# Decode attention scores as 32-row products on keys turned by VectorE, with half of the paged latents gathered by index

## What is computed

```
kv latent cache (N_POOL pages, 128 tokens, 256), rope cache (N_POOL, 128, 32), page_table (8, 32), all float32
ckv, kr  = pages of the 8 sequences            # 8 x 4096 tokens x (256 + 32)
q_lat    = q_nope (8 seq, 8 tok, 6 heads, 64) . w_uk            -> (.., 256)
s_past   = (q_lat . ckv + q_rope . kr) * scale                  # over 4096 tokens
s_new    = the same against the 8 new tokens, causal mask
pr       = softmax([s_past, s_new])
o_lat    = pr . [ckv, ckv_new];   out = o_lat . w_uv
```

## Time and profile before

| | us |
|---|---|
| median of 3 runs (2025.14 to 2026.98) | 2026.8 |
| the profiled execution | 2029.75 |
| its span | 2028.1 |
| decode stage, first transpose (465.3) to the next stage's first DMA (733.3) | 268 |
| PE busy over the span | 1869.0 (92%) |
| mean granted TensorE clock, of full speed | 0.946 |

### The profile page before, as it was taken

One profiled execution on the slowest core, in us unless ns is written; L12 is line 12 of the kernel. 1 busy time (PEld: TensorE's weight loads), 2 busy tenths in 40 slices (PEclk: granted clock), 3 DMA queues, 4 the chain that ended last, 5 costly groups with the idle time before them and its releaser, 6 DMA issues. The chain is left out here.

```text
span 2028.1 us, 39649 instructions
## 1 busy us (share of the span) xinstructions
PE 1869.0 (92%) x16034; PEld 1641.6 (81%) x16034; DVE 978.9 (48%) x1800; ACT 513.8 (25%) x1064; POOL 255.0 (13%) x440
## 2 busy tenths in 40 slices
PE   5999998998999965999898979999999999999997
PEld 5999984665666632888746979999999999999996
DVE  6232426673455547544245335545545535445455
ACT  5111123542323333223124321111111111111113
POOL 1000004324444302000002210000000000000000
PEclk8999998998999966999867989999999999999999
DMA  7111113104555400000031111021021121110202
GB/s 231 53 42 53 40 43 83 31 10 130 154 155 153 124 25 0 4 4 4 18 132 53 32 32 42 22 73 37 27 63 42 31 64 32 42 53 24 64 21 111
DMA packets 148258, 119.19 MB, mean 59 GB/s; under 512 B 22900, under 2 KB 136298, under 8 KB 147805
## 3 DMA queue, kind: packets, MB, share of 16 engines
q1 hardware_dynamic: 138189, 97.35, 16.4%
q0 software_dynamic: 9744, 18.78, 3.4%
q10 hardware_dynamic: 144, 0.52, 0.1%
HBM read 102.81 MB, written 11.44 MB: 56 GB/s over the span
## 5 line engine op out<-in xcount | busy, mean ns | idle before, releaser
L202 PE MATMUL bank<-normed2T_hi,w_hi 128*128 128x384 f32 (+1 forms) x1056 | 346.0, 328 | 4.3 <-DVE w_lo L492 4.3
L203 PE MATMUL bank<-normed2T_hi,w_lo 128*128 128x384 f32 (+1 forms) x1056 | 345.7, 327 | 0.0
L204 PE MATMUL bank<-normed2T_lo,w_hi 128*128 128x384 f32 (+1 forms) x1056 | 345.7, 327 | 0.0
L202 PEld LDWEIGHTS bank<-normed2T_hi,w_hi 128*128 128x128 f32 x1056 | 199.1, 189 | 5.5 <-DVE w_lo L492 5.5
L203 PEld LDWEIGHTS bank<-normed2T_hi,w_lo 128*128 128x128 f32 x1056 | 199.0, 188 | 0.0
L204 PEld LDWEIGHTS bank<-normed2T_lo,w_hi 128*128 128x128 f32 x1056 | 199.0, 188 | 0.0
L202 PE MATMUL bank<-inner_hi,w_hi 128*128 128x384 f32 (+1 forms) x528 | 174.4, 330 | 10.2 <-DVE w_lo L492 7.1
L492 DVE TENSOR_TENSOR w_lo<-work,w_hi 128x1024 fp32r<-128x1024 f32 (+2 forms) x120 | 118.6, 989 | 131.1 <-ACT w_hi L487 129.9
L204 PE MATMUL bank<-inner_lo,w_hi 128*128 128x384 f32 (+1 forms) x528 | 174.1, 330 | 0.0
L203 PE MATMUL bank<-inner_hi,w_lo 128*128 128x384 f32 (+1 forms) x528 | 173.6, 329 | 0.0
L202 PE MATMUL bank<-normedT_hi,w_hi 128*128 128x384 f32 (+3 forms) x480 | 157.6, 328 | 5.5 <-DVE w_lo L492 5.5
(11 more groups left out here) (411 smaller groups left out, 3348.3 us busy)
## 6 DMA issues: line engine op xcount, KB each, us to landing
work<-in_w_up_dram SPq DMA_DIRECT2D x44, 512.0 KB, 3.8
residualT<-in_cache_kv_latent_dram SPq DMA_DIRECT2D x80, 128.0 KB, 2.5
residualT<-in_cache_kv_latent_dram POOLq DMA_DIRECT2D x80, 128.0 KB, 2.6
work<-in_w_in_dram SPq DMA_DIRECT2D x19, 512.0 KB, 3.8
work<-in_w_down_dram SPq DMA_DIRECT2D x32, 256.0 KB, 2.8
weight_ring<-in_cache_kv_latent_dram POOLq DMA_DIRECT2D x48, 128.0 KB, 2.7
weight_ring<-in_cache_kv_latent_dram SPq DMA_DIRECT2D x48, 128.0 KB, 2.5
residualT<-residual_spill SPq DMA_DIRECT2D x1, 4352.0 KB, 15.0
```

Of the source, the lines that this page charges most:

```text
L202: pe.matmul(out, w[0], x[0], start=first, stop=False)
L203: pe.matmul(out, w[1], x[0], start=False, stop=False)
L204: return pe.matmul(out, w[0], x[1], start=False, stop=last)
```

## The change

- **Keys.** PE no longer transposes the keys. DVE `turn_keys(j)` transposes each slot of load j in place of it, in blocks of 32x32, SBUF to SBUF: two instructions of [128, 1024] and two of [128, 128] per load, two loads ahead of the step that uses them.
- **Scores.** With 32x32 blocks turned, the 32 partitions of a page hold 32 of the 256 latents of its tokens at a time. `dscores` becomes 9 blocks (8 of latents, 1 of rope) x 4 pages q x 2 halves f = 72 products with 32 rows of contraction, 64 columns of queries and 128 columns of keys; page q writes bank q, and successive steps use different 128-column parts of the banks. The small step has 9 x 2 x 2 = 36 such products of 32 columns.
- **Queries.** They are stored as `q_blk`: each block of 32 latents repeated in all four groups of 32 partitions, scaled by SCALE already. `w_uk` is spread so that PE forms the repeated blocks: 48 products of 64 rows by 128 columns in place of 12.
- **Softmax.** DVE forms the negated maximum in one instruction, so the instruction L1450 goes. `copy_weights` and `copy_part` move from DVE to ACT; ACT's key copies go.
- **Loads.** SP issues only the four latent pages of half 0. POOL gathers, with indirect DMAs of 128 rows each, the latents of half 1 (4 KB a row) and the rope rows of both halves (512 B a row): three instructions per load in place of seven. Row numbers are computed on POOL in four small instructions at the start of the attention stage. The gather of rope rows waits for `k_t` of load j - 5, that of latents for `do_mm` as before. In the attention stage POOL's share of the early loads goes to the rounds q = 8 to 11: one gather in even rounds, two in odd ones.
- The table of pages goes to all partitions; some small copies of new keys are replaced by one transpose.

The core of the diff:

```diff
+        def load_pages(eng, j):
+            x, g = loads[j]
+            for q in range(4):
+                at_ = x * NPAGE + 4 * g + q
+                page = eng.value_load(pages[0:1, at_:at_ + 1], min_val=0, max_val=NPOOL - 1)
+                eng.dma_start(kslot[2 * (j % NL)][32 * q:32 * q + 32],
+                              kv_pages[bass.ds(page, 1)].rearrange("a p c -> (a p) c")).then_inc(s_k[0][j % NL], 16)
+        def gather_latents(pool, j, f):
+            x, g = loads[j]
+            b = x + NX * f
+            pool.indirect_dma_start(kslot[2 * (j % NL) + f], None, kv_rows,
+                                    bass.IndirectOffsetOnAxis(row_at[:, b, g:g + 1], 0)).then_inc(s_k[f][j % NL], 16)
...
             @block.gpsimd
             def _(pool):
-                all_loads(pool, 1)
+                for j in range(EARLY, len(loads)):
+                    if j >= NL:
+                        pool.wait_ge(k_t, 2 * (j - NL) + 2)
+                    for f in range(2):
+                        gather_ropes(pool, j, f)
+                    if j >= NL:
+                        pool.wait_ge(do_mm, step_of(j - NL) + 1)
+                    for f in (1,):
+                        gather_latents(pool, j, f)
...
+                    for b in range(KB):
+                        for q in range(4 if g < NG else 2):
+                            rows = slice(32 * q, 32 * q + 32)
+                            for f in range(2):
+                                out = PS[q][HD * f:HD * f + HD, P * (s % 2):P * (s % 2) + P]
...
+                                last = pe.matmul(out, q_blk[rows, b, x, f, :], keys, start=(b == 0),
+                                                 stop=(b == KB - 1), skip_group_check=True)
...
                 for s in range(NSTEP):
                     x, g = steps[s]
-                    following = s + 1 < NSTEP and steps[s + 1][1] < NG and steps[s + 1]
                     dscores(s)
                     if g == JOINED and x >= 1:
                         turn_joined(x - 1)
-                        pe.wait_ge(j_cp, x)
-                    if following:
-                        turn_keys(following[0] * NG + following[1], 0)
                     if s >= 1:
-                        dvalues(s - 1, 0)
-                    if following:
-                        turn_keys(following[0] * NG + following[1], 1)
+                        dvalues(s - 1)
                     turn_weights(s)
-                    if s >= 1:
-                        dvalues(s - 1, 1)
...
+                def turn_keys(j):
                     if j >= 2:
                         dve.wait_ge(ds_mm, step_of(j - 2) + 1)
+                    for f in range(2):
+                        slot = 2 * (j % NL) + f
+                        dve.wait_ge(s_k[f][j % NL], (64, 16)[f] * (j // NL + 1))
+                        dve.transpose(key_t[:, j % 2, f, 0:4 * RANK], kslot[slot])
+                        dve.wait_ge(s_kr2[f][j % NL], 16 * (j // NL + 1))
+                        dve.transpose(key_t[:, j % 2, f, 4 * RANK:KT], krr[:, slot, :]).then_inc(k_t, 1)
...
+                dve.wait_ge(s_nm, 16)
+                turn_keys(0)
+                turn_keys(1)
                 for s in range(NSTEP):
                     x, g = steps[s]
-                    following = s + 1 < NSTEP and steps[s + 1][1] < NG and steps[s + 1]
                     softmax_max(s)
-                    for half in range(2):
-                        if following:
-                            copy_keys(following[0] * NG + following[1], half)
-                    copy_weights(s)
-                    if s >= 1:
-                        copy_part(s - 1)
+                    if g < NG and x * NG + g + 2 < len(loads):
+                        turn_keys(x * NG + g + 2)
```

More of the change, by code:

```diff
@@ L984, in _ @@
                 pool.wait_ge(s_kr[1], 1)
+                pool.wait_ge(s_pg, 16)
+                for r in range(4):
+                    rows = slice(32 * r, 32 * r + 32)
+                    nc.gpsimd.tensor_scalar(row_at[rows], pages[rows].rearrange("p (b g r) -> p b g r", b=NB, r=4)[:, :, :, r],
+                                            32.0, C("page_row")[rows], ALU.mult, ALU.add).then_inc(s_ra, 1)
+                pool.wait_ge(s_ra, 4)
                 for q in range(NQ):
@@ new lines, in _ @@
+                for m in range(3):
+                    pe.wait_ge(wu_cp[m], 1)
+                    for b in range(KB - 1):
+                        for f in range(2):
+                            r = slice(HD * f, HD * f + HD)
+                            last = pe.matmul(PS[2 * m + f][:, b * NS:(b + 1) * NS],
+                                             w_uk_b[r, m, b].rearrange("p q c -> p (q c)"), qn[r, m, SEQ:T],
+                                             start=True, stop=True)
+                    last.then_inc(ql_mm, 1)
@@ L1252, in _ @@
-                act.wait_ge(s_q0, 2)
-                latent_queries(nc.scalar.copy, 1)
+                act.wait_ge(wu_t, 4)
+                spread_w(nc.scalar.copy, 1).then_inc(wu_cp[1], 1)
+                rope_queries(nc.scalar.mul, (0, 1))
+                for m in range(3):
+                    act.wait_ge(ql_mm, m + 1)
+                    latent_queries(nc.scalar.mul, 2 * m + 1)
         if upto == "queries":
@@ L1287, in build, with scores_of @@
         y_mm = sem("decode_values_ready")
-        with nc.Block() as block:
-            def all_loads(eng, f):
-                for j in range(EARLY, len(loads)):
-                    if j >= NL:
-                        eng.wait_ge(do_mm, step_of(j - NL) + 1)
-                    load_rows(eng, j, f)
+        def scores_of(s):
+            x, g = steps[s]
+            n, w = (4, P) if g < NG else (2, 32)
+            by_bank = banks8[:, 0:n * 512].rearrange("p (q w) -> p q w", q=n)
+            return by_bank[:, :, P * (s % 2):P * (s % 2) + w]
+        with nc.Block() as block:
             @block.sync
```

322 lines of the change are left out of this document (131 added, 191 removed).

## The result

The changed kernel takes 1998.2 us (median; 1996.7 to 2001.4) where the kernel before took 2026.9 in the same comparison: a ratio of 0.9862 with a 95% interval of 0.9845 to 0.9879. That is 28.7 us less, where 74 had been forecast. The profiled execution has a span of 1999.6 us.

A forecast was written before the change was run, and what follows sets the result against it. PE was taken to bound decode, busy 64.31 of 66 us. Steps -75, start of decode -3 and +1, queries +2.5, attention +0.5 gave -74 us: median 2026.8 to 1953 us, range 1936 to 2016.

The forecast's parts named there:

- Scores: Decode stage on PE: 144 records of 128 columns at 14.2 ns, 2.1 us per step, between 1.9 and 3.9.
- four tiles at once: Rival on decode scores: no more than four tiles work together, scores 3.9 us, PE's step 6.3, 1995 us; chance 0.13.
- the rows don't overlap: Slower rival on scores: only two column halves work at once, 7.7 us, step 10.1, 2115 us; 0.05 shared with falling clock.
- PE's step of 4.5 us: Full decode step by PE alone: scores 2.1, change of shape 0.1, chain 1.77, and 0.53 us.
- POOL sets the pace: Rival in decode: gathers of 1.6 to 2.3 us; at 1.96 the step is 6.2 us, 1991 us; chance 0.13.
- the gathers cost more than a step: Slower rival in decode: at 2.6 us per gather on POOL the step is 8.1 us, 2055 us; chance 0.09.
- The step of 5.0 us: Full decode step: 4.8 us mean from PE and DVE's joins plus 0.2 for mutual waits; 7.34 before, saving 75 us.
- the rival in which the clock falls: Slower rival: PE's idle times drop its clock to 1.2 GHz, step near 9 us, 2080 us; 0.05 shared with non-overlapping rows.
- Queries stage: PE does 96 records, not 24, two overlapping, 5.1 us; with spread and end copies +2.5 us (0 to +5).
- Start of decode: DVE turns load 0 in 3.0 us before first scores, previously at 6.2: -3 us; slow clock at start +1.
- Attention stage: POOL's row numbers and early gathers: round 9 needs 3.8 us against 3.58, +0.5 us (up to +4).
- Wrong it is if PE waits on DVE: Sign against the forecast: PE waiting on DVE in plain decode steps, or scores above 2.5 us.

## Why the prediction was right and wrong

The direction, and most of the prices, were right. 1998.2 us lies in the range, in its upper part, and 45 us above the point. The change gained 28.7 us of the 74 forecast.

- **Scores.** 2.1 us were forecast, for eight tiles working at once and a record every 14.2 ns. Without loads, and without the gathers alone, 144 records start within 2.05 us: the price was right for the array. In the changed kernel, beside the gathers, it was 2.34 in the median of the steps without a stop, 0.3 more, and the prediction had nothing for that. The rivals "four tiles at once" and "the rows don't overlap" are out. So is, for these tiles, the 25 ns of the Trainium skill that the prediction had weighed against the trace.
- **PE's step of 4.5 us.** The shortest steps without loads took 4.50 us, and two loads at once 9.65: right as what PE can do.
- **DVE.** 1.22 and 0.29 us were forecast for a turning. All 40 + 24 large ones have 1218 and 1219 ns, and the small ones 269:

```profile
L1430 DVE STREAM_TRANSPOSE work<-residualT 128x1024 f32<-128x1024 f32 x40 | 48.7, 1218 | 2.8 <-DMA residualT<-in_cache_kv_latent_dram 2.0 <-PEq L160 0.8
L1432 DVE STREAM_TRANSPOSE work<-residualT 128x128 f32<-128x128 f32 x64 | 17.2, 269 | 0.0
L878 POOL DMA_INDIRECT residualT<-in_cache_k_rope_dram,mixedT x64 | 61.6, 963 | 27.2 <-issue 15.6 <-POOLq L160 8.3 <-DVE work L1432 3.4
```

- **POOL.** A gather was put at 1.3 us (0.5 to 2.4); it takes 0.96, with 0.30 before the next: 3.8 us per load. The rivals "POOL sets the pace" and "the gathers cost more than a step" are out; what the gathers do to PE is a way that no rival had. All gathers of the decode stage took 0.94 to 1.20 us, though DVE turned keys beside them.
- **The step of 5.0 us: the step that failed.** The sum went through PE's work, DVE, SP, POOL and the DMA engines, and added 0.2 us for their entanglement. It had no term for the arrival of PE's instructions, of which the change takes 328 per step where there were 122. The forecast was 32 x 5.0 + 3 x 3.5 = 170.5 us from the first scores to the last small step's, and 212.6 came: 42 of the 45 us. Stops for instructions are 22.9 of the 42. Scores that start 0.3 us slower beside the gathers make some 9 (an estimate, 32 x 0.3, from the steps at full clock with and without them). The rest, some 10, is left for the lower clock and the waits for ACT; no run separates these. So the step failed by what its sum put at nothing: above all the arrival of instructions, then the slower start of the scores and the lower clock.
- **The clock.** 1.00 was forecast for the stage. A part of the rival in which the clock falls came true: 0.90 and 0.97 in the two windows, and 0.50 for 32 us of the 212.6, 12 of them at the start of the stage and the others each behind a long stop of PE.
- **Queries stage: mis-sized.** 96 x 53 ns = 5.1 us were forecast because alternating halves of the rows would overlap. 96 records took 10.50 us at a granted clock of 0.50, 109 ns each; in another kernel the same 96 took 5.58 at 1.00, 58 ns each. So one follows the other at either clock. That is weights of 128 columns and no overlap of the halves, as for the 24 records of the earlier trace rows, which should have been taken as they were. The Trainium skill, TensorE: Matmul & The Clock Gate, section "LDWEIGHTS (loading the stationary operand)", says that a weight load's time goes by its columns and not by its rows, columns/1.2 in ns: 107 ns for 128. At half clock the trace agrees; at full clock it shows 58. With that rule the stage would have been put at 10.3 us. The error is 5.4 us. Some of it came back, since the stage began 0.8 us earlier than in the kernel before, where half a microsecond later was forecast. The first scores came at 474.3 where the terms of the sum give 471.5; with the 42 us of the steps that makes up the 45.
- **Start of decode.** The first scores stood 2.8 us behind DVE's first instruction of the stage (474.32 and 471.51), with 3.0 forecast: right.
- **Attention stage.** The round after the ninth came 3.79 us behind it (379.96 to 383.75), against 3.58 in the earlier trace rows; 3.8 had been worked out. The end of the stage was not later for it.
- **What it would take.** "Wrong it is if PE waits on DVE" looked for the wait in the wrong place. After its first scores PE waited on other engines for 4.1 us of the stage, and for its instructions for 22.9.

## What to carry to other kernels

Count instructions as a resource. A change that trades few large products for many small ones must also be checked against the arrival of instructions, and not only priced at the rate at which the engine starts them. In the kernels here PE stopped for instructions where it used 256 of them per 4.2 to 5.4 us, and hardly (0.8 us of 160) at 7.3. The profile shows it before the change: in the recurrence stage of the kernel before (861 to 977 us, 27 packets, 4.2 us apart) PE already waited 6.5 us for instructions. When that is the bound, widen the products (256 columns in place of 128) even at the price of buffers; another order gave nothing back. A split that is meant to change the number of instructions alone can change the pace of the products too: read their pitch in a stretch without a stop before the difference is put down to anything. And don't put gathers of GpSimd at the end of a stage.

## What the runs showed of the hardware

- PE receives its instructions by DMA in packets of 16 KB, 256 instructions, each of which took 0.9 to 1.4 us in the changed kernel's decode stage. When PE has used up those that have landed it stops, and goes on 1.2 to 1.7 us after the end of the next packet (122 stops of over 0.3 us in nine traces). In the decode stage of the changed kernel they came 4.94 us apart, 4.23 without any loads, 4.29 without the gathers alone, 4.53 without the pages alone; the closest pair was 3.3 us apart. In the recurrence stage of the kernel before, between 861 and 977 us, they came 4.2 us apart in the mean.
- 32-row by 64-column tiles: 144 records of 128 columns start within 2.05 us, 14.2 ns each; of 256 columns 64 start within 1.61 us, 25.6 ns each. Two products of 128 columns one after the other on the same tile: 128 records start within 2.55 us, 20 ns each, and 160 within 3.2 to 3.4.
- GpSimd's gathers slow these starts: 2.31 to 2.34 us for the 144 in the median beside them, 2.05 or 2.06 in all 16 such steps without them.
- 64-row tiles with weights of 128 columns don't overlap (58 ns a record at full clock, 109 at half); with weights of 64 columns 192 took 4.73 us.
- A 32x32 turning by VectorE of [128, 1024] four-byte values takes 1.22 us. A gather of 128 rows costs GpSimd 0.94 to 1.20 us, whether its rows have 0.5 or 4 KB.
- With gathers as GpSimd's last work in a stage, the next stage began 4.1 us after the last of them was issued and 7.35 us after DVE's last work, in place of 0.78 after it; with the sync engine's page loads under way it was 0.78 again.
- Open: when the next packet is asked for, why the page traffic delays it, and why gathers slow PE's starts.
